# A transformer kernel in which query tiles and half of an output projection move in between the attention steps

## The reference

```
def second_block(x, ...):
    h = x
    for layer in range(2):
        hn = rms_norm(h, attn_norm[layer])
        if layer == 0: h = h + swa_sink_mixer(hn, a_w_qkv, a_b_qkv, a_sinks, a_w_o, a_b_o, rel_table)
        else:          h = h + nsa_mixer(hn, b_w_in, ..., b_w_o, rel_table)
        h = h + swiglu(rms_norm(h, ffn_norm[layer]), ffn_w_gu[layer], ffn_w_down[layer])
    return rms_norm(h, final_norm)

def swa_sink_mixer(h, w_qkv, b_qkv, sinks, w_o, b_o, rel_table):
    qkv = h @ w_qkv + b_qkv               # 1024 query columns, 128 key, 128 value
    q, k, v = ...                         # 16 query heads of 64 in 2 groups; 2 key and 2 value heads
    o = banded_attention(q, k, v, A_WINDOW, rel_table, sinks)
    return o.reshape(B, S, ATTN_WIDTH) @ w_o + b_o

    # inside banded_attention, for each block of 128 queries
    m = jnp.maximum(jnp.max(s, axis=-1, keepdims=True), sk)     # sk: the sinks
    e = jnp.exp(s - m)
    p = e / (jnp.sum(e, axis=-1, keepdims=True) + jnp.exp(sk - m))
    return jnp.einsum('bhgqs,bshd->bqhgd', p, vn)
```

## Time and profile before

| | |
|---|---|
| time, median of 3 runs | 1135.58 us (1132.31 to 1136.16) |
| profiled execution | 1134.58 us, its span 1131.6 us |
| PE busy | 1063.2 us (94%) |
| DVE, ACT, POOL busy | 693.1, 563.4, 206.5 us |
| mean granted TensorE clock | 0.971 of full |
| layer 0, tiles of q, k, v | to 479.3 us of the span |
| layer 0, attention | 479.3 to 518.2 us |
| layer 0, output projection | 518.2 to 541.4 us |
| layer 1, end of attention | 905.7 us |

### The profile page before, as it was taken

One profiled execution on the slowest core, in us unless ns is written; L12 is line 12 of the kernel. 1 busy time (PEld: TensorE's weight loads), 2 busy tenths in 40 slices (PEclk: granted clock), 3 DMA queues, 4 the chain that ended last, 5 costly groups with the idle time before them and its releaser, 6 DMA issues.

```text
span 1131.6 us, 23550 instructions
## 1 busy us (share of the span) xinstructions
PE 1063.2 (94%) x8892; PEld 1034.1 (91%) x8892; DVE 693.1 (61%) x1334; ACT 563.4 (50%) x1083; POOL 206.5 (18%) x221
## 2 busy tenths in 40 slices
PE   5888988999999998999999999999799999999998
PEld 5778888999999997989999999999788899999997
DVE  5478664777775446755666674477445366666643
ACT  3354456456664334675544453357456554444431
POOL 5000000053341212004211113300000051111230
PEclk9888999999999999999999999999789899999999
DMA  9433332455556556504566657664500055665740
GB/s 278 84 96 93 115 111 76 135 165 174 181 181 208 185 186 149 177 11 112 149 184 181 179 167 202 209 159 141 184 1 2 1 150 160 180 182 161 215 143 38
DMA packets 225602, 161.38 MB, mean 143 GB/s; under 512 B 7379, under 2 KB 222776, under 8 KB 225530
## 3 DMA queue, kind: packets, MB, share of 16 engines
q1 hardware_dynamic: 222592, 154.23, 45.3%
q0 software_dynamic: 2544, 6.04, 3.2%
q10 hardware_dynamic: 394, 0.13, 0.1%
HBM read 158.28 MB, written 2.10 MB: 142 GB/s over the span
## 4 chain that ended last, share of the span: by engine, by line
PE 81%; DVE 8%; ACT 5%; issue 2%; DMA 2%; POOL 1%; SPq 0%; DVEq 0%; ACTq 0%; POOLq 0%
PE bank L585 22%; PE bank L587 22%; PE bank L586 22%; PE bank L836 4%; PE bank L824 2%; PE bank L581 2%; PE bank L808 2%; PE bank L809 2%; DVE w_lo L1474 1%; ACT work L1256 1%; DMA raw<-w_in_in 1%; DVE big L1531 1%; ACT w_hi L1082 1%; ACT big L1270 1%; PE bank L736 1%
## 5 line engine op out<-in xcount | busy, mean ns | idle before, releaser
L1474 DVE TENSOR_TENSOR w_lo<-raw,w_hi 128x1024 fp32r<-128x1024 f32 (+2 forms) x281 | 356.8, 1273 | 222.0 <-ACT w_hi L1082 220.1
L585 PE MATMUL bank<-hh,w_hi 128*128 128x256 f32 x1384 | 398.0, 288 | 16.1 <-ACT work L1227 8.1
L586 PE MATMUL bank<-hl,w_hi 128*128 128x256 f32 x1384 | 394.9, 285 | 0.0
L587 PE MATMUL bank<-hh,w_lo 128*128 128x256 f32 x1384 | 394.7, 285 | 0.0
L1082 ACT ACTIVATE w_hi<-raw 128x1024 fp32r<-128x1024 f32 (+2 forms) x281 | 299.0, 1081 | 169.7 <-PE bank L587 159.8
L585 PEld LDWEIGHTS bank<-hh,w_hi 128*128 128x128 f32 x1384 | 267.7, 193 | 20.7 <-issue 12.7
L586 PEld LDWEIGHTS bank<-hl,w_hi 128*128 128x128 f32 x1384 | 267.8, 194 | 0.1
L587 PEld LDWEIGHTS bank<-hh,w_lo 128*128 128x128 f32 x1384 | 267.8, 193 | 0.0
L585 PE MATMUL bank<-hidh,w_hi 128*128 128x256 f32 x672 | 188.7, 281 | 1.2 <-POOL hidl L2134 1.1
L586 PE MATMUL bank<-hidl,w_hi 128*128 128x256 f32 x672 | 188.2, 280 | 0.0
L587 PE MATMUL bank<-hidh,w_lo 128*128 128x256 f32 x672 | 188.2, 280 | 0.0
(11 more groups left out here) (257 smaller groups left out, 1334.0 us busy)
## 6 DMA issues: line engine op xcount, KB each, us to landing
raw<-ffn_w_gu_in SPq DMA_DIRECT2D x88, 512.0 KB, 5.0
raw<-w_ff_in SPq DMA_DIRECT2D x64, 512.0 KB, 4.2
raw<-w_in_in SPq DMA_DIRECT2D x26, 512.0 KB, 6.2
raw<-ffn_w_down_in SPq DMA_DIRECT2D x32, 384.0 KB, 4.1
raw<-ffn_w_down_in SPq DMA_DIRECT2D x32, 320.0 KB, 3.4
raw<-b_w_in_in SPq DMA_DIRECT2D x14, 512.0 KB, 4.7
raw<-a_w_qkv_in SPq DMA_DIRECT2D x10, 512.0 KB, 4.5
raw<-w_out_in SPq DMA_DIRECT2D x8, 512.0 KB, 4.5
```

The source lines that it names most:

```text
L585: pe.matmul(o, ah, bh, start=start, stop=False)
L586: pe.matmul(o, ah, bl, start=False, stop=False)
L587: return pe.matmul(o, al, bh, start=False, stop=stop)
L1474: dve.tensor_tensor(tile_view(w_lo, n), raw_view(n), tile_view(w_hi, n).bitcast(F32), ALU.subtract)\
```

## The change

In layer 0 PE makes the four query tiles of the first key group, the key tile, the value tile and one more query tile, and then the other three query tiles between the steps of units 4 and 5. The output projection is cut in two halves over its input: the first half (chunks 0 to 3, which units 4 and 5 give) is made as 8 tiles of 12 matmuls between the steps of units 6 and 7, in banks 0, 2 and 3, and DVE adds each to `x`; the second half, 8 tiles of 12 matmuls, follows the attention, with the bias. The weights of this projection lie in tiles of 4 chunks by 128 columns, four to a slot. The `keep_busy` calls of layer 0's attention are gone. `Y_BANK` is bank 6, in place of 0, for all units of the program: bank 0 is now a projection bank during layer 0's attention. The row maxima and sums have three buffers in place of two, and `soften(u)` waits for each pair's transposes apart.

```
-    for j in range(5):
-        plain("a_w_qkv_2", 0, 0, KC, 256 * j, 256)
+    for c0 in (0, 256, 1024, 512, 768):
+        plain("a_w_qkv_2", 0, 0, KC, c0, 256)
...
+        if layer == 0:
+            for kc0 in (0, 4):
+                for j in range(2):
+                    plain("a_w_o_2", 0, kc0, 4, 512 * j, 512)
...
-        S_BANK, T_BANK, V_BANK, Y_BANK = 2, 6, 1, 0
+        S_BANK, T_BANK, V_BANK, Y_BANK = 2, 6, 1, 6
...
+        LAST_HALF = {"out": 0, "wo0": KC, "wo1": 0}
...
             def square_projection(name, xh, xl, ready):
                 for fc in range(KC):
-                    m = ST[name] + fc
+                    m = ST[name] + LAST_HALF[name] + fc
                     tile_ready(m)
                     open_bank(fc % 2, (x_done, 8 * RES[name] + fc + 1))
-                    feature_tile(m, half(fc % 2), xh, xl, ready=ready if fc == 0 else None).then_inc(tiles_done, 1)
+                    feature_tile(m, half(fc % 2), xh, xl, LAST_HALF[name] // 2,
+                                 ready=ready if fc == 0 else None).then_inc(tiles_done, 1)
...
+                def first_half(fc, b):
+                    m = ST["wo0"] + fc
+                    tile_ready(m)
+                    open_bank(b, (x_part, fc + 1))
+                    feature_tile(m, half(b), yh, yl, ready=(lambda k: (y_done, 6)) if fc == 0 else None)\
+                        .then_inc(tiles_done, 1)
...
+                    projected(4, 0, "sk")
+                    projected(5, 1, "svT")
+                    projected(6, 0, "sq4")
+                    to_rows("sv", 0, 0, P, 1, ev["svT"])
                     pe.wait_ge(*ev["sk"])
-                    pe.wait_ge(*ev["sv"])
-                    units(4, 7)
+                    scores(4)
+                    projected(7, 0, "sq5")
+                    scores(5)
+                    transposes(4, (0, 1))
+                    projected(8, 0, "sq6")
+                    transposes(4, (2, 3))
+                    pe.wait_ge(*ev["sv"])
+                    values(4)
+                    projected(9, 0, "sq7")
+                    transposes(5, (0, 1))
+                    pe.wait_ge(*ev["sq7"])
+                    scores(6)
+                    transposes(5, (2, 3))
+                    rows_to_columns(4)
+                    values(5)
+                    transposes(6, (0, 1))
+                    scores(7)
+                    transposes(6, (2, 3))
+                    rows_to_columns(5)
+                    values(6)
+                    first_half(0, 0)
+                    first_half(1, 2)
+                    transposes(7, (0, 1))
+                    first_half(2, 3)
+                    transposes(7, (2, 3))
+                    rows_to_columns(6)
+                    first_half(3, 0)
+                    values(7)
+                    first_half(4, 2)
+                    first_half(5, 3)
+                    first_half(6, 0)
+                    rows_to_columns(7)
+                    first_half(7, 2)
...
+                def add_half(fc, b):
+                    prefetch(ST["wo0"] + fc + 4)
+                    dve.wait_ge(tiles_done, ST["wo0"] + fc + 1)
+                    dve.tensor_tensor(x[:, fc, :], half(b), x[:, fc, :], ALU.add).then_inc(x_part, 1)
```

More of the change, by code:

```diff
@@ L812, in scores, with transposes @@
                     close_bank(mm, f"S{u}{k}", S_BANK + k)
-            def transposes(u):
+            def transposes(u, groups=(0, 1, 2, 3)):
                 U = UNITS[u]
                 rows = min(P, U["nk"])
-                for k in range(4):
+                for k in groups:
                     pe.wait_ge(p_ready, 4 * u + k + 1)
@@ L973, in _ @@
[L973 to L980 removed]
+                    for j in range(4):
+                        projected(j, j % 2, f"sq{j}")
+                    projected(4, 0, "sk")
@@ new lines, in _ @@
+                    first_half(2, 3)
[8 more added lines that the diff above has]
+                    first_half(7, 2)
+                else:
+                    for j in range(8):
+                        projected(j, j % 2, f"nq{j}")
@@ L1376, in _, with query_high @@
                 n = ST[("qkv", "nsa")[layer]]
-                for j in range(8):
-                    tile(n + j)
+                def query_high(m, j, b):
+                    tile(m)
                     for e in range(2):
@@ L1391, in _ @@
                                     cols[r, COL["a_b_qkv_2"] + 8:COL["a_b_qkv_2"] + 9]).then_inc(q_hi, 1)
-                    tile(n + 9)
+                    tile(n + 5)
                     act.activation(vT[:, 0, :], psum[1][:, 0:T], ACT.Copy).then_inc(ev_act, 1)
-                    prefetch(n + 12)
-                    for u in range(4, 8):
-                        unit(u)
-                else:
+                    query_high(n + 6, 4, 0)
+                    exps(4, 0)
+                    exps(4, 1)
@@ L1398, in _ @@
+                    take_transposed(7, 2)
+                    take_transposed(7, 3)
+                    take_columns(6)
+                    prefetch(ST["wo0"] + 10)
+                    take_columns(7)
+                else:
+                    for j in range(8):
+                        query_high(n + j, j, j % 2)
                     for kv in range(2):
@@ L1952, in _, with query_low @@
                 n = ST[("qkv", "nsa")[layer]]
-                for j in range(8):
-                    tile(n + j)
+                def query_low(m, j, bank, his):
+                    tile(m)
                     for e in range(2):
                         a, b = slice(HD * e, HD * e + HD), slice(HD * (1 - e), HD * (1 - e) + HD)
-                        dve.wait_ge(q_hi, 18 * layer + 2 * j + e + 1)
+                        dve.wait_ge(q_hi, his + e + 1)
                         hi = qs[a, 2 * j + e, :].bitcast(F32)
```

158 lines of the change are left out of this document (112 added, 46 removed).

## The result

The changed kernel takes 1149.51 us (median of 4 executions, 1146.05 to 1152.88) against 1134.81 us for the kernel before (4 executions beside it, 1132.31 to 1136.16): ratio 1.0132, 95% interval 1.0096 to 1.0167. The prediction was 1139.5 us, with a range up to 1144. The direction is as forecast; the size isn't: 14.7 us slower and not 5. Run again in a later set (`after2`) the changed kernel took 1146.33 us, ratio 1.0108 (1.0078 to 1.0138), 11.8 us slower. The mean granted clock over its executions was 0.961 in the first set and 0.964 in the second; the kernel before has 0.968 to 0.970 in sets of 11 to 29.

A forecast was written before the change was run, and what follows sets the result against it. PE, busy 94% of the span, was taken as the bound. 1134.58 - 1.9 (layer 0) + 2.7 (bank 6 waits) + 1.8 (two keep_busy tails) + 2.5 (clock) = 1139.7, stated as 1139.5 us, range 1133.5 to 1144.

The forecast's parts named there:

- bank 6: Columns in bank 6 outside layer 0: 2.7 us for six PE waits plus 1.8 for two keep_busy calls.
- the waits of 0.45 us: First block and layer 1: PE's step into columns waits for ACT's copy six times, 2.7 us in all.
- the first tail: End of unit 3: keep_busy must wait until the columns are read and delays the projection by 0.9 us.
- The second tail: End of unit 19: keep_busy after the columns are read delays the projection by 0.9 to 1.8 us; 0.9 taken.
- the wait for POOL: Layer 0's projection, second half: DVE's instructions block POOL, so PE waits 4.9 us for its sum of squares.
- the clock behind it: Layer 0's first feed-forward tiles: the granted clock falls after PE's long wait, costing 2.5 us, from 0 to 6.0.
- rival 1: No change that can be told: POOL less blocked or clock stays up, bank waits stand; 1134.6 us, chance 0.25.
- rival 2: Faster: other waits absorb bank 6's, POOL takes 1.52 us a chunk, clock stays up; 1130.1 us, chance 0.08.
- layer 0: Attention and output projection with the moved tiles: POOL's sum lets PE go at 539.5, not 541.4; gain 1.9 us.
- The seven foreseen waits in the attention: Layer 0's attention: PE waits for ACT, low parts and y_low(7), 0.4 to 1.1 us each, 5.0 in sum.
- rival 4: Layer 0's attention: ACT's fixed order holds PE up, doubling the 5.0 us of waits; 1144.7 us, chance 0.15 with rival 3.
- Rival 3: Slower: clock stays low longer after the POOL wait and at unit 19's tail; 1144.1 us, chance 0.15 with rival 4.

The follow-up runs named there:

- b_w32: Kernel before with pads ahead of the weight tiles and behind hl, putting weights and all moving operands at the same place modulo 256 bytes; 1138.86 us, ratio 1.0042.
- b_work96: Kernel before with 96 unused bytes per partition ahead of the work region, placing its activations as in the changed kernel; 1134.59 us, ratio 1.0007.
- b_y6: Kernel before with the columns in bank 6 in units 0 to 3 and 8 to 19, bank 0 in layer 0; 1141.82 us, ratio 1.0057.
- a_work32_y0: Changed kernel with 32 unused bytes ahead of the work region and the columns back in bank 0 outside layer 0; 1131.28 us, ratio 0.9957 to before.
- a_tail7: Changed kernel with 32 unused bytes ahead of the work region and series-end keep_busy in bank 7, columns still in bank 6; 1135.27 us, ratio 1.0003 to before.
- b_h64: Kernel before with hh and hl moved to +64 bytes against the weights' tiles, all else at its place modulo 256; 1123.87 us, ratio 0.9885.
- best: Changed kernel with columns in bank 0 outside layer 0, hh and hl at +32, hidh and yh at +160 against the weights; 1122.85 us, ratio 0.9887 to before.
- b_h128: Kernel before with hh and hl moved to +128 bytes against the weights' tiles, all else at its place modulo 256; 1129.11 us, ratio 0.9939.

## Why the prediction was wrong

**The step that failed** is that everything outside the named places was costed at nothing. The three buffers that grew were read as buffers, not as 96 bytes that move `hidh`, `hidl`, `yh` and `yl`, the operands of 2592 of the matmuls. That term is 5.7 us by the pitch and 4.8 by b_w32, though only 0.8 by b_work96. The starts of consecutive matmuls in before would have shown 0.1175 beside 0.1200 for the same form, a difference that no row of the prediction explains.

**Mis-sized: bank 6.** 4.5 us foreseen; 5.2 by the traces, 6.5 (3.1 to 9.9) by b_y6, 7.4 to 10 by a_work32_y0. The mechanisms were right, the waits of 0.45 us and the 0.9 of the first tail too. The second tail was put at 0.9, out of 0.9 to 1.8, and is 1.7: its eight matmuls run at the lower level of the clock, as the prediction had seen in before and not taken. What the times have beyond the traces was not pinned down; b_y6 and a_tail7 have a lower mean clock than before, 0.967.

**Right: the wait for POOL.** 4.23 us against 4.9 foreseen; the sum was ready 15.5 us after the first chunk, foreseen 16.5. Which of POOL's steps is blocked was wrong, and made no difference. Right too: the clock behind it (2.5 foreseen, 2.4 in the trace of after, 1.4 to 3 in six traces), which means rival 1's "the clock stays up" and rival 2 fell.

**Nearly right, in part by luck: layer 0.** -1.9 us foreseen, -1.0 in the trace. Of the 1.9, 1.65 were the half clock of before at 482.7 us. It went, but another one fell into the first query tiles, about 1.5 us, which the prediction's "if no half clock falls into the new order" had left out. The second half of the projection started 1.7 us later than laid out (524.56 us; 520.7 and 2.1 of shift were foreseen), and the 1.9 us less that PE waits in that half (1.3 and 4.23, foreseen 2.5 and 4.9) made up for it. The seven foreseen waits in the attention are there within 0.3 us, so rival 4 falls.

**Rival 3** (1144.1, clock down longer) had the right direction for the rest, but not its mechanism: behind the wait for POOL the clock of after is 0.85 over 20 us, 3 us lost and not 6. Adding up: 4.8 (or 5.7) for the place, 6.5 to 7.4 for bank 6, and for the new layer 0 with its clock: a_work32_y0 is 4.4 us faster than before, of which its shorter pitch (0.1187 against 0.1190, 2.3 us) isn't layer 0's, so -2.1. The sum is 9 to 11 us; measured are 11.8 and 14.7. With the 0.8 us of b_work96 for the place it is 5 us. What is left, 1 to 5 us or more, was not pinned down. The lower mean clock of the changed kernel, and the 4.5 us between two executions of it in layer 1's attention, say where it is likely to be; no run here shows why its clock falls more.

## What to carry to other kernels

Before an edit that changes the size of any buffer, see which tensors it moves, and keep each matmul's moving operand off the weights' place modulo 256 bytes (32 and 64 bytes beside it were best here); read the pitch of consecutive matmuls, not their duration. A wait of the matrix engine may have to be paid twice, the second time in its clock (a wait of 4.2 us cost 1.4 to 3 us more), so filler work belongs into the wait. It must not itself depend on what is waited for: at the end of unit 19 filler that did stood 1.7 us in the way. A window of one trace compared with a window of another has to start at the same instruction in both. Work moved out of the end of a stage helps only as far as the engine that sums up behind it can follow.

## What the hardware showed that was not expected

- The pitch of a 128x256 matmul at the full clock depends on the distance between moving operand and weights in SBUF, modulo 256 bytes (or 512, see above). Means by operand and block or layer, over all kernels here: +0: 0.1196 to 0.1201; +32: 0.1166 to 0.1178; +64: 0.1143 to 0.1178; +128: 0.1186 to 0.1188; +160: 0.1173 to 0.1199; +224: 0.1183 to 0.1187. The spread has a further cause that was not found: in layer 1 b_h64 has 0.1198 for `hidh` and `hidl`, best 0.1174 at the same address, and in the q, k and v tiles of layer 0 of b_h128 `hh` and `hl` at +128 have 0.1199.
- POOL and DVE, both with two operands in SBUF, delay each other: POOL's multiplication 0.94 or 1.48 us instead of 0.72, DVE's split of 128x1024 1.75 instead of 1.30 and that of 128x512 1.23 instead of 0.69.
- A matmul row of the trace lasts 0.28 us at any pitch, so busy times and means hide all of this: PE's busy share was 94% before and 93% after.
